# Joining the triangular inverses of the RWKV block on 64x64 quadrants of the tensor array, interleaved head by head

## The reference, cut to what matters

```python
rwkv7_recurrence(r_h, d_h, k_h, v_h, kk, a_h)   # 8 heads x 64, 512 tokens, state 64x64 per head
```

## Time and profile before

| | us |
|---|---|
| median of 3 runs | 2079.82 |
| the three runs | 2074.15, 2081.5, 2079.82 |
| the profiled execution | 2085.79 |
| span of its instructions | 2084.2 |
| PE busy in the span | 1943.0 (93%) |
| DVE busy in the span | 1578.5 (76%) |
| the join pipeline, first T to last J | 743.0 to 797.5 |

### The profile page before, as it was taken

How to read it: one execution, slowest core, us unless ns; L and a number is a source line. 1 busy time by engine, 2 the same in 40 slices (tenths; PEclk the granted TensorE clock), 3 DMA queues, 4 the chain that set the end, 5 groups by cost and what they waited for, 6 DMA issues and landing times.

```text
span 2084.2 us, 26814 instructions
## 1 busy us (share of the span) xinstructions
PE 1943.0 (93%) x9199; PEld 1552.9 (75%) x9199; DVE 1578.5 (76%) x1612; ACT 1214.7 (58%) x1235; POOL 435.2 (21%) x385
## 2 busy tenths in 40 slices
PE   7999888878989987889999999999999999999997
PEld 5766555666757777678888888888888888888884
DVE  5663353764363726688999999999999999999996
ACT  5645564324343332136777777777777777777773
POOL 4435542010060161124101111111111111111110
PEclk9999998989975988789999999999999999999998
DMA  7435431433100101469999999999999999999994
GB/s 203 152 123 171 152 127 56 146 59 92 40 1 0 31 21 49 156 232 317 377 393 397 392 399 391 394 386 395 385 392 389 392 387 393 383 398 387 389 373 154
DMA packets 180400, 525.04 MB, mean 252 GB/s; under 512 B 34530, under 2 KB 52018, under 8 KB 180338
## 3 DMA queue, kind: packets, MB, share of 16 engines
q1 hardware_dynamic: 156882, 458.27, 58.1%
q0 software_dynamic: 21376, 65.95, 11.0%
q10 hardware_dynamic: 2080, 0.01, 0.1%
HBM read 499.06 MB, written 25.12 MB: 252 GB/s over the span
## 4 chain that ended last, share of the span: by engine, by line
PE 54%; DVE 2%; issue 0%; POOLq 0%; POOL 0%; DVEq 0%
PE banks L3357 51%; PE banks L3345 3%; PE banks L3351 1%; PE banks L3421 0%; DVE expert_weights L3695 0%; DVE x_tokens L3691 0%; DVE weights_lo L3491 0%; DVE x_tokens L3702 0%; DVE x_tokens L3574 0%; PE banks L3478 0%; PE banks L3442 0%; PE banks L3412 0%; DVE u_lo L3527 0%; DVE rows_lo L3521 0%; DVE member L3554 0%
## 5 line engine op out<-in xcount | busy, mean ns | idle before, releaser
L3491 DVE TENSOR_TENSOR weights_lo<-expert_weights,weights_hi 128x2048 fp32r<-128x2048 f32 x384 | 877.0, 2288 | 65.7 <-ACT weights_hi L3731 61.5
L3731 ACT ACTIVATE weights_hi<-expert_weights 128x2048 fp32r<-128x2048 f32 x384 | 739.7, 1928 | 263.5 <-PE banks L3357 252.2
L3357 PE MATMUL banks<-weights_hi,rows_hi 128*128 128x512 f32 x1024 | 319.1, 393 | 0.0
L3357 PE MATMUL banks<-weights_hi,rows_lo 128*128 128x512 f32 x1024 | 315.5, 389 | 0.0
L3357 PE MATMUL banks<-weights_lo,rows_hi 128*128 128x512 f32 x1024 | 273.8, 389 | 0.0
L3357 PEld LDWEIGHTS banks<-weights_hi,rows_hi 128*128 128x128 f32 x1024 | 189.8, 188 | 44.9 <-issue 7.3
L3357 PEld LDWEIGHTS banks<-weights_hi,rows_lo 128*128 128x128 f32 x1024 | 192.3, 188 | 40.4
L3357 PEld LDWEIGHTS banks<-weights_lo,rows_hi 128*128 128x128 f32 x1024 | 192.3, 188 | 39.9
L3357 PE MATMUL banks<-weights_hi,u_hi 128*128 128x512 f32 x512 | 161.3, 396 | 1.4 <-DVE u_lo L3527 1.4
L3357 PE MATMUL banks<-weights_hi,u_lo 128*128 128x512 f32 x512 | 158.4, 390 | 0.0
L3357 PE MATMUL banks<-weights_lo,u_hi 128*128 128x512 f32 x512 | 137.8, 391 | 0.0
(11 more groups left out here) (596 smaller groups left out, 2826.5 us busy)
## 6 DMA issues: line engine op xcount, KB each, us to landing
expert_weights<-in_exp_w SPq DMA_DIRECT2D x384, 1024.0 KB, 10.1
enter_rows<-in_ada_w POOLq DMA_DIRECT2D x24, 1024.0 KB, 5.7
w_in_landing<-in_w_in SPq DMA_DIRECT2D x16, 384.0 KB, 3.3
second_landing<-in_w_in SPq DMA_DIRECT2D x12, 512.0 KB, 3.6
x_tokens<-in_x SPq DMA_DIRECT2D x8, 512.0 KB, 6.5
w_in_landing<-in_w_in SPq DMA_DIRECT2D x8, 512.0 KB, 3.6
enter_w_landing<-in_w_out SPq DMA_DIRECT2D x8, 512.0 KB, 5.5
leave_w_landing<-in_w_o SPq DMA_DIRECT2D x8, 512.0 KB, 9.7
```

What stands on the lines that cost most here:

```text
L3357: last = nc.tensor.matmul(c.banks[:, bank + n, :], left[:, 2 * q + kk, :], right[:, q, kk * FF + n * 512:kk * FF + (n + 1) * 512], start=s ...
L3491: nc.vector.tensor_tensor(w_lo[:, ch % SPLIT, :], c.raw[:, ch % RAW if place is None else place, :], w_hi[:, ch % SPLIT, :], ALU.subtract) ...
L3731: nc.scalar.activation(w_hi[:, ch % SPLIT, :], c.raw[:, ch % RAW if place is None else place, :], ACT.Copy).then_inc(hi_ready.sem, 1)
```

## The change

Lower, Z and J now use the 64x64 quadrant that holds their data: lower reads partitions 0 to 63 and writes 0 to 63, Z reads 0 to 63 and writes 64 to 127, J reads 64 to 127 and writes 0 to 63. They stand behind all upper products of the iteration and alternate head by head: lower of unit i-1, Z of i-2, J of i-3, for n = 0 to 3. The waits of the three stand together ahead of the first. z and xa are no longer filled with zeros.

```diff
-                nc.gpsimd.memset(inverse, 0.0)
-                nc.gpsimd.memset(z, 0.0)
-                nc.gpsimd.memset(xa, 0.0).then_inc(x_cleared.sem, 1)
+                nc.gpsimd.memset(inverse, 0.0).then_inc(x_cleared.sem, 1)
...
-                            last = nc.tensor.matmul(c.banks[:, 2, n * 64:(n + 1) * 64], inverse[:, g, h, :],
-                                                    y[:, (i - 1) % 2, n, 0:64], start=True, stop=True)
-                        last.then_inc(x_ready.sem, 1)
...
-                            last = nc.tensor.matmul(c.banks[:, 3, n * 64:(n + 1) * 64], nt[:, g, h, :],
-                                                    xa[:, i % 2, n, :], start=True, stop=True)
-                        last.then_inc(z_ready.sem, 1)
...
-                            last = nc.tensor.matmul(c.banks[:, 4, n * 64:(n + 1) * 64], z[:, (i - 3) % 2, n, :],
-                                                    inverse[:, g, h, 64:P], start=True, stop=True)
-                        last.then_inc(j_ready.sem, 1)
+                    if 4 <= i <= units + 2:
+
+                        pe.wait_ge(j_copied.sem, i - 3)
+                    for n in range(4):
+                        if 1 <= i <= units:
+                            g, q = step_of(i - 1)
+                            lower = nc.tensor.matmul(c.banks[low, 2, n * 64:(n + 1) * 64], inverse[low, g, 4 * q + n, low],
+                                                     y[low, (i - 1) % 2, n, low], start=True, stop=True)
+                            if n == 3:
+                                lower.then_inc(x_ready.sem, 1)
+                        if 2 <= i <= units + 1:
+                            g, q = step_of(i - 2)
+                            left = nc.tensor.matmul(c.banks[high, 3, n * 64:(n + 1) * 64], nt[low, g, 4 * q + n, high],
+                                                    xa[low, i % 2, n, :], start=True, stop=True)
+                            if n == 3:
+                                left.then_inc(z_ready.sem, 1)
+                        if 3 <= i <= units + 2:
+                            g, q = step_of(i - 3)
+                            join = nc.tensor.matmul(c.banks[low, 4, n * 64:(n + 1) * 64], z[high, (i - 3) % 2, n, low],
+                                                    inverse[high, g, 4 * q + n, high], start=True, stop=True)
+                            if n == 3:
+                                join.then_inc(j_ready.sem, 1)
```

More of the change, by code:

```diff
@@ L2598, in rwkv_core @@
     rows_of = lambda j: slice(64 * j, 64 * j + 64)
+    low, high = rows_of(0), rows_of(1)
     out_bank = lambda t, h=0: c.banks[:, 2 if t == TT - 1 and h >= 4 else (7, 1)[t % 2], :]
@@ L2809, in _ @@
                                              start=True, stop=True)
-                            last = nc.tensor.matmul(c.banks[:, 2, n * 64:(n + 1) * 64], inverse[:, g, h, :],
-                                                    y[:, (i - 1) % 2, n, 0:64], start=True, stop=True)
-                        last.then_inc(x_ready.sem, 1)
                     if 2 <= i <= units + 1:
-                        g, q = step_of(i - 2)
                         pe.wait_ge(x_taken.sem, i - 1)
-                        if i >= 3:
-                            pe.wait_ge(z_copied.sem, i - 2)
@@ L2820, in _ @@
-                        for h, f, j, n in heads_of(q):
-                            last = nc.tensor.matmul(c.banks[:, 3, n * 64:(n + 1) * 64], nt[:, g, h, :],
-                                                    xa[:, i % 2, n, :], start=True, stop=True)
-                        last.then_inc(z_ready.sem, 1)
                     if 3 <= i <= units + 2:
-                        g, q = step_of(i - 3)
                         pe.wait_ge(z_copied.sem, i - 2)
-                        if i >= 4:
-                            pe.wait_ge(j_copied.sem, i - 3)
```

## The result

| | before | changed |
|---|---|---|
| median, us | 2081.97 (20 runs, 2066.58 to 2097.66) | 2069.85 (20 runs, 2051.24 to 2081.09) |
| ratio of the times | | 0.9934 (95% 0.9906 to 0.9962) |
| profiled execution, us | 2085.79 | 2078.05 (span 2076.4) |
| first T to last state update, us | 54.42 | 41.83 |
| last state update to the next block, us | 27.30 | 29.86 |

The change is worth 0.66%, 13.7 us (7.9 to 19.6). The forecast was 2069.8 and 10.0 us of gain. The median came out there, but the pipeline itself gained 12.6 us, not 10.0: the forecast let two of the three products queue behind each other, and rival (a), all three at once, is what the trace shows.

A forecast was written before the change was run, and what follows sets the result against it. PE bounds up to the last state update at 799, DVE behind it. Iterations 3 to 8 give 8.7 us, plus 0.56, 0.3 and 0.69, less 0.2 for waits: 10.0 off 2079.8, so 2069.8; range 2064.5 to 2076.

The forecast's parts named there:

- rival (a): Pipeline: all three quadrants run at once, body 0.45 us, 13.0 us gained, time 2066.8; chance 0.27.
- Side by side: Lower, Z, J: row halves run together, lower and Z in the same rows do not; body 0.90 us an iteration.
- staggered variant: Form of rival (a): passes start only in program order, staggered by one; body 0.67 us, 11.8 us gained, time 2068.
- Load and matmul in a quadrant: Short passes of lower, Z, J: load about 54 ns, matmul about 0.054 us; overlapped, about 0.056 us a pass.
- Changing the form: Between full and quadrant passes, once an iteration: 0.33 us for the round trip, ends 0 and 0.4.
- idle loader of 0.1 to 0.3 us: Sign in the profile after: weight loader idle 0.1 to 0.3 us before the first full load behind each group.
- The new wait: Upper of the next unit waits for DVE's x_taken; just fits, 0.2 us charged over iterations 2 to 5.
- Rival (b): Pipeline: one stream, or PE fed too slowly; gain 7.5 us (2072.3), or 6.4 us (2073.4) at 0.062 a pass; chance 0.17.
- Rival (c): Quadrant group: load not hidden, quadrants don't overlap, 0.107 us a pass; 1.9 us slower, 2081.7; chance 0.05.
- Rival (d): Pipeline: quarter-filled array lets the clock fall to 1.2 GHz; time over 2100; chance 0.02.
- Behind 799 everything shifts as a whole: Behind the last state update at 799: everything moves earlier together, DVE's stretch there staying 25 us long.
- The fills on POOL: Zero fills 45 us before the pipeline: dropping them gains zero; 1.5 us if they were not hidden.

The follow-up runs named there:

- e10: The kernel before, profiled a second time with no change: first T to last state update 54.21 us, against 54.42 in its first profile.
- e4: The changed kernel, profiled a second time with no change: first T to last state update 41.45 us, tail 30.12 us.
- e1: Changed kernel with all lower, then all Z, then all J, in place of head by head: iteration 3.55 us against 3.10, first T to last state update 44.87.
- e9: Changed kernel with Z and J ahead of upper and lower behind it, one more change of form per iteration: iteration 3.79 us against 3.10, pipeline 46.39.
- e5: Changed kernel with Y and upper in quadrants too: iteration 2.47 us, pipeline 35.68; median 2066.21 us, ratio 0.9881 to the kernel before.
- e6: The changed kernel again, timed and profiled a third time: median 2067.35 us over ten runs, ratio 0.9904 to the kernel before; pipeline 41.62, tail 27.29.
- e3: New order with 64-row moving operands but all 128 stationary columns, against the kernel before: iteration 4.30 us against 4.86, pipeline 51.03 against 54.42.
- e7: Changed kernel plus three extra full-form products ahead of the last u, into an unread bank: pipeline 41.44 us, tail 27.29, single run 2053.05.
- e12: The same kernel as e7, changed kernel plus three extra products, run once more: pipeline 41.44 us, tail 27.30, time 2068.33.

## Why the prediction was right, and where it was not

The time was right (2069.8 forecast, 2069.85 measured) and so was its place, between T and the last s. The gain there was forecast at 10.0 us and measured at 12.6 (12.4 to 13.0 over all pairs of profiles). Term by term, from the starts of T and u in the two traces:

| term | forecast | measured |
|---|---|---|
| 24 short passes side by side | 0.90 | 0.46 |
| changing the form, there and back | 0.33 | 0.35 |
| new wait of upper for x_taken | 0.2 in all | 0.12 in each of 3, 4 and 5; in iteration 2 it fell from 0.34 to 0.20 |
| iteration 0 | 0 | -0.2 (3.00 to 3.21; it scatters, 2.79 in e10 and 2.82 in e4) |
| iteration 1 | +0.3 | +0.14 (3.64 to 3.50) |
| iteration 2 | +0.56 | +1.12 (4.30 to 3.18) |
| iterations 3 to 5 | 3 x 1.45 | 5.26 (3 x 1.75) |
| iterations 6 and 7, u to u | 2 x 1.45 | 3.73 (14.52 to 10.79) |
| iterations 8 and 9, u to u | 1.45 + 0.69 | 2.56 (11.67 to 9.11) |
| behind the last u | 0 | 0 (2.73 to 2.75) |

**The step that failed** is "Side by side". It took 0.90 us because no row showed that two quadrants in the same rows run together, and that was the middle one of its three values. They do, 0.007 us apart, and 0.46 is what rival (a) said (0.45). Seven iterations (2 to 8) have this body, 0.44 us shorter each: 3.1 us more than forecast. Iteration 0 took back 0.2, the wait in 3 to 5 another 0.16 and the changes of form 0.02 in each of the seven, 0.14; that leaves 12.6. Iteration 1 and its way out came as forecast, 0.14 there and 0.14 off the wait in iteration 2, and so did iteration 9, 0.69. (a) priced the gain at 13.0, and it is the mechanism here. Its staggered variant, with passes that start only in program order, is out: the body would be 0.67, and e1 shows passes that start ahead of earlier ones.

**Load and matmul in a quadrant** were built from other shapes, as 0.056 us a pass. Measured 0.058. The fixed part of a load and the price of a column, read off loads of 6, 32 and 128 columns, gave 84 + 54 = 138 ns for 64 columns; the loads of line 2821 take 0.13 to 0.14 us.

**Changing the form** was read from a place with other shapes as 0.33. Measured 0.35, here and in e9. The idle loader of 0.1 to 0.3 us, named as a sign of it, is 0.07 ahead of T (761.70 + 0.135 to 761.90); the rest of the way out is the load that nothing hides. The Trainium skill (TensorEngine Tiling, Key Properties) says that a change of mode drains the engine; these rows agree, and 0.20 in and 0.15 out is what it costs in this kernel.

**The new wait** was forecast as just fitting, 0.2 in all, with 0.11 to 0.2 us of Z and J behind the last lower. Since the three run side by side, next to nothing stands there, and the wait is 0.12 in each iteration that has nothing but T and Y between. It grew because another term was better than forecast, and in e5 it is what stops the next gain (0.35).

**Rival (b)**, one stream or PE fed too slowly, is out: 24 short passes are taken in 0.46 us, 0.019 each, far below the 0.062 of the earlier trace rows and below the 0.058 at which passes of one quadrant follow each other in e1. Those transposes are slow for another reason, which no run here looked at. The Trainium skill (TensorE: Matmul & The Clock Gate, section "Wait — 56ns, not 53.3ns?") names the same 62 ns for each matmul, and only where the hardware's own decoding of matmuls is off, a condition that the prediction left out and that no trace here shows. In this group the trace does not agree, and the measurement decides.

**Rival (c)**, slower, needed 0.098 us a pass where 0.019 were measured. **Rival (d)**, the clock, did not happen in the pipeline (1.00 in the stretch). A small relative of it did, in the tail of 2 of the changed kernel's 3 profiles, for 2.6 and 2.8 us; the forecast's step "Behind 799 everything shifts as a whole" holds in e6 (27.29) and fails in the other two. **The fills on POOL** were put at zero. From the block's first instruction to the first T it is 58.0 us before and 57.8 after, so they were hidden.

**Why the median still met the forecast.** The stages give 12.6 less up to 2.6 in the tail, 10 to 13 us. The medians differ by 12.1 and the ratio says 13.7 (7.9 to 19.6), so neither excludes the other, and the baseline of the forecast was 2.2 us below the median of 20 runs. 2069.85 is thus partly luck: two errors of some 2 us with opposite signs. The scatter of the runs, 30 us, is larger than both, and no set of runs of this size can separate 10 from 13. The stages could.

## What to carry to other kernels

Where only half of the rows and half of the columns of a small fp32 product matter, put it on the quadrant that holds its data and alternate products of different quadrants pass by pass; the row half alone gave 3.4 us here and the column half 9.4, since the load gets cheaper with columns and not with rows (0.11 a pass in e3, 0.058 in quadrants), and since products in the same rows then run beside each other too. Gather all such products in one group for each round, since a change of form costs 0.35 us here, and then look for the hand-over that comes next. When the runs of a kernel scatter by more than the change is worth, compare the stages of two traces between the same instructions, and look in the clock row of the stages ahead before a fast run is believed.

## What the runs showed of the hardware that was not expected

- Three 64x64 quadrants, two of them in the same rows with different moving data, start passes about 0.007 us apart and run at once, 8 passes each at 0.058 us.
- PE starts passes out of program order over quadrants, but only a little: three passes ahead when eight of one quadrant stand in a row (760.85 against 761.02 in e1).
- The change between 128x128 and 64x64 forms costs 0.20 us in and 0.15 us out, 0.35 a trip, in the changed kernel as in e9.
- Stages at 1.2 GHz come and go in the same kernel on the same code: 27 or 65 us in the stage ahead (e7 and e12), 44.2 against 62.3 us for the same instructions, and 10 us behind the last state update, worth 2.6 to 2.9.
